# RWKV-7 chunk scan: shifted decay sum, key norm one interval ahead with a rectifier as its bound, products in halves

## What is computed

```python
kk = heads(k * k_k)
kk = kk / jnp.maximum(jnp.sqrt(jnp.sum(kk * kk, axis=-1, keepdims=True)), 1e-12)
k = k * (1.0 + (a - 1.0) * k_a)
def step(s, inp):
    r_t, w_t, k_t, v_t, aa_t, bb_t = inp          # aa = -kk, bb = kk * a
    sa = jnp.einsum('bhij,bhj->bhi', s, aa_t)
    s = s * w_t[:, :, None, :] + sa[..., None] * bb_t[:, :, None, :] + v_t[..., None] * k_t[:, :, None, :]
    return s, jnp.einsum('bhij,bhj->bhi', s, r_t)
# then per head: (y - mean) * rsqrt(var + eps) * ln_w + ln_b, plus (sum(r * k * r_k)) * v, times g, times w_o
```

## Time and profile before

| what | value |
|---|---|
| median of 3 runs | 3407.89 us (3406.33 to 3411.68) |
| the profiled execution's own time | 3415.54 us |
| its span, first to last instruction | 3413.7 us |
| mean granted PE clock | 0.965 of full |
| busy over the span | PE 90%, PEld 86%, DVE 50%, ACT 35%, POOL 29% |

### The profile page before, as it was taken

How to read it: one execution, slowest core, us unless ns; L and a number is a source line. 1 busy time by engine, 2 the same in 40 slices (tenths; PEclk the granted TensorE clock), 3 DMA queues, 4 the chain that set the end, 5 groups by cost and what they waited for, 6 DMA issues and landing times.

```text
span 3413.7 us, 73904 instructions
## 1 busy us (share of the span) xinstructions
PE 3072.6 (90%) x32214; PEld 2938.2 (86%) x32214; DVE 1694.1 (50%) x1713; ACT 1209.4 (35%) x1399; POOL 984.7 (29%) x545
## 2 busy tenths in 40 slices
PE   5999799999999997699968888887989999999996
PEld 5888699999999997699966777776979999999996
DVE  6455654544455456102116666663364445445555
ACT  4634322221222224433326777775132221112222
POOL 2222222222222223213313444444132222222221
PEclk9999899999999998799979999998999999999998
DMA  2111011111111110332231221222101111111111
GB/s 97 42 41 39 25 38 44 44 43 43 43 43 43 42 40 25 117 141 84 90 97 32 68 67 53 66 56 88 44 25 44 44 44 45 44 44 44 43 44 61
DMA packets 92154, 185.88 MB, mean 54 GB/s; under 512 B 33504, under 2 KB 56544, under 8 KB 91872
## 3 DMA queue, kind: packets, MB, share of 16 engines
q1 hardware_dynamic: 84960, 154.80, 14.5%
q10 hardware_dynamic: 6912, 26.84, 1.9%
HBM read 145.07 MB, written 36.53 MB: 53 GB/s over the span
## 4 chain that ended last, share of the span: by engine, by line
PE 75%; DVE 11%; ACT 8%; POOL 3%; issue 2%; DMA 1%; ACTq 0%; SPq 0%; DVEq 0%; POOLq 0%
PE PS L1112 66%; PE PS L1274 8%; DVE T L1543 3%; ACT T L460 2%; DVE X L1533 2%; ACT L460 2%; DVE T L1533 1%; DVE G L1533 1%; POOL HL L897 1%; DVE HL L1533 1%; ACT X L460 1%; PE PS L1230 1%; ACT UV L460 1%; POOL X L1002 1%; DVE NN L1533 1%
## 5 line engine op out<-in xcount | busy, mean ns | idle before, releaser
L897 POOL TENSOR_TENSOR WL<-RAW,WH 128x1024 fp32r<-128x1024 f32 x204 | 498.1, 2441 | 1562.4 <-ACT WH L460 1558.7
L1112 PE MATMUL PS<-HH,WH 128*128 128x364 f32 x3456 | 773.7, 332 | 79.5 <-POOL HL L897 42.2
L1112 PE MATMUL PS<-HH,WL 128*128 128x364 f32 x3456 | 769.9, 331 | 0.0
L1112 PE MATMUL PS<-HL,WH 128*128 128x364 f32 x3456 | 767.5, 331 | 0.0
L1112 PEld LDWEIGHTS PS<-HH,WH 128*128 128x128 f32 x3456 | 602.3, 190 | 94.1 <-issue 50.2
L1112 PEld LDWEIGHTS PS<-HH,WL 128*128 128x128 f32 x3456 | 608.0, 190 | 0.0
L1112 PEld LDWEIGHTS PS<-HL,WH 128*128 128x128 f32 x3456 | 606.1, 190 | 0.0
L1543 DVE SCALAR_TENSOR_TENSOR T<-T,FP 128x1092 f32<-128x1092 f32 x192 | 456.4, 2377 | 6.8
L1533 DVE TENSOR_TENSOR X<-PS,X 128x1092 f32<-128x1092 f32 x224 | 290.3, 1296 | 272.3 <-PE PS L1112 267.9
L460 ACT ACTIVATE WH<-RAW 128x1024 fp32r<-128x1024 f32 x204 | 216.6, 1062 | 408.1 <-PE PS L1112 387.7
L1112 PE MATMUL PS<-PH,WH 128*128 128x364 f32 x1344 | 301.3, 333 | 53.4 <-DVE X L1533 38.2
(11 more groups left out here) (157 smaller groups left out, 3399.6 us busy)
## 6 DMA issues: line engine op xcount, KB each, us to landing
RAW<-weights SPq DMA_DIRECT2D x204, 512.0 KB, 3.5
scratch<-T ACTq DMA_DIRECT2D x32, 546.0 KB, 2.9
scratch<-SR ACTq DMA_DIRECT2D x16, 546.0 KB, 2.9
X<-xT SPq DMA_DIRECT2D x8, 546.0 KB, 7.7
yT<-T SPq DMA_DIRECT2D x8, 546.0 KB, 2.9
T<-scratch_m SPq DMA_DIRECT2D x8, 512.0 KB, 4.1
LW<-scratch SPq DMA_DIRECT2D x16, 192.0 KB, 2.6
KK<-scratch SPq DMA_DIRECT2D x16, 192.0 KB, 2.6
```

The source lines that it names most:

```text
L897: pool.tensor_tensor(out, full, hi, ALU.subtract).then_inc(*t.made(event))
L1112: mm = pe.matmul(acc[:, j, :], a, b[:, j * CW:(j + 1) * CW], start=(i == 0 and q == 0), stop=(i == len(blocks) - 1 and q == 2))
```

## The change

- **Key norm one interval ahead.** `scaled_key`, `key_square`, `key_squares`, the lower bound, `norm_ln` and `norm_exp` work on batch job+3 (guard `has_k`) in place of job+2. All engines start at interval -3, SP at -4, loading batch job+4.
- **Its bound as a rectifier on ACT.** `floor` (DVE, max with 1e-24) becomes `above_floor` on ACT: Relu(x - 1e-24), and Ln adds the 1e-24 again.
- **Exclusive sum as a shifted inclusive one.** Z2 gets 65 columns per chunk, the first one filled with ones at the start of the scan. `removal` reads columns 0 to 63, `receptance` 1 to 64. `exclusive` on POOL and `decay_before` on ACT go.
- **Small vectors once.** PP and PQ of all pairs are loaded at the start of the program (16 DMAs); `one_less` is done once, on DVE.
- **Affine on ACT.** The scale and shift of the group norm move from DVE to ACT, after `norm_exp`.
- **Products in halves.** `solved` is cut by bank (keys, then values) with `means` between; `lower` is cut by bank with `link(4)` and `left_times(5)` between. `solved_values` waits for the new semaphore k_wv.
- **Bank 2 by its last reader.** `sums` waits for whoever read bank 2 last, in place of waits written out.
- **New orders** of the calls on all four engines; ACT's puts rectifier, Ln (key), Ln (group) and Exp (group), Exp (key) together.

The core of the diff:

```diff
-        Z2 = at("Z2", [NCH, CHUNK], o); o += PACK * 4
+        Z2 = at("Z2", [NCH, CHUNK + 1], o); o += NCH * (CHUNK + 1) * 4
...
+            for q, tile in enumerate((PP, PQ)):
+                for f in range(KT):
+                    sp.dma_start(tile[:, f, :], io["pair_vec"][q][f]).then_inc(*t.made("dma_pair"))
...
-                if job + 3 < JOBS:
-                    f, b = divmod(job + 3, NB)
-                    if job >= 0:
-                        sp.wait_ge(*t.at("k_g", 8 * (job + 1)))
-                        sp.wait_ge(*t.at("k_bonus", job + 1))
-                    sp.dma_start(PP[b][:, :], io["pair_vec"][0][f]).then_inc(*t.made(f"dma_in{b}"))
+                if job + 4 < JOBS:
+                    f, b = divmod(job + 4, NB)
+                    if job >= -1:
+                        sp.wait_ge(*t.at("k_g", 8 * (job + 2)))
+                        sp.wait_ge(*t.at("k_bonus", job + 2))
...
+                def above_floor():
+
+                    if has_k:
+                        act.wait_ge(*t.next("s_kk", 2))
+                        run(X2[:, klo:khi], PS[:, 2, 0:khi - klo], ACT.Relu, "k_max", bias=-1e-24)
...
+                def affine():
+
+                    if has_n:
+                        y = flat(Y)[:, na * CHUNK:nz * CHUNK]
+                        act.wait_ge(*t.next("k_pn"))
+                        run(y, y, ACT.Identity, "k_pt", scale=PQ[:, nf, 0:1], bias=PQ[:, nf, 1:2])
...
                 scaled_key()
                 spread_out()
-                one_less()
+                key_square()
                 key_factor()
-                key_square()
                 solved_keys()
                 solved_values()
                 decay_in()
                 turned(1)
                 growth()
+                centred_square()
+                above_floor()
                 norm_ln()
+                values()
+                turned(2)
+                group_ln()
+                group_exp()
+                turned(3)
                 norm_exp()
-                decay_before()
-                centred_square()
-                turned(2)
-                values()
-                group_ln()
-                turned(3)
-                group_exp()
+                affine()
                 keys()
                 turned(4)
                 outputs_y()
                 turned(5)
...
-                unit_plus()
-                exclusive()
-                receptance()
-                grown_key()
                 unit_key()
                 taken_key()
+                unit_plus()
                 grown_taken()
+                grown_key()
+                receptance()
                 normed()
...
                 spread()
                 powers()
-                solved()
+                solved(0)
+                means()
+                solved(1)
                 seed()
                 key_squares()
                 moves_and_left(2)
-                means()
+                fresh_out()
+                grow(2)
+                value_turn()
                 fresh_state()
-                grow(2)
-                fresh_out()
+                variances()
+                left_times(3)
                 link(0)
-                left_times(3)
+                products(0)
                 link(1)
-                value_turn()
-                variances()
-                link(2)
                 grow(3)
-                link(3)
-                products(0)
-                link(4)
-                left_times(4)
                 bonus_sums()
                 products(1)
+                link(2)
+                left_times(4)
+                key_turn()
+                link(3)
                 grow(4)
-                key_turn()
+                lower(0)
+                link(4)
+                left_times(5)
+                lower(1)
                 link(5)
-                left_times(5)
-                lower()
                 grow(5)
```

More of the change, by code:

```diff
@@ L416, in interval @@
                             sp.dma_start(dst, SE[q][:, :]).then_inc(*t.made("dma_state"))
-            for job in range(-3, JOBS - 2):
+            for job in range(-4, JOBS - 2):
                 interval(job)
@@ L738, in scaled_key @@
                 def scaled_key():
[L740 to L746, removed]
-                        run(PP[pb][:, 3:4], PP[pb][:, 1:2], ACT.Copy, "k_om", scale=-1.0, bias=1.0)
+                    if has_k:
+                        act.wait_ge(*t.next(f"dma_in{kb}", 10 if kb == NB - 1 else 5))
+                        run(X1[:, klo:khi], KK[:, klo:khi], ACT.Copy, "k_kk", scale=PP[:, kf, 0:1])
                 def key_square():
-                    if has_p:
-                        run(X2[:, lo:hi], X1[:, lo:hi], ACT.Square, "k_sq")
+                    if has_k:
+                        run(X2[:, klo:khi], X1[:, klo:khi], ACT.Square, "k_sq")
                 def spread_out():
@@ L804, in key_factor @@
                     if has_p:
-                        run(X3[:, lo:hi], AA[:, lo:hi], ACT.Identity, "k_ka", scale=PP[pb][:, 1:2], bias=PP[pb][:, 3:4])
+                        run(X3[:, lo:hi], AA[:, lo:hi], ACT.Identity, "k_ka", scale=PP[:, pf, 1:2], bias=PP[:, pf, 3:4])
                 def centred_square():
@@ L866, in interval @@
                 turned(5)
-            for job in range(-2, JOBS + 1):
+            for job in range(-3, JOBS + 1):
                 interval(job)
@@ L1260, in interval @@
                 pa, pz = BATCHES[pb]
+                ka, kz = BATCHES[(job + 3) % NB]
                 na, nz = BATCHES[(job - 1) % NB]
@@ L1914, in interval @@
                 one_more()
+                centred()
+                grown(1)
                 key()
-                grown(1)
-                weighted()
-                floor()
-                mask(2)
-                transfer()
-                centred()
-                reading()
-                grown(2)
+                mask(2)
+                reading()
+                removal()
+                grown(2)
+                transfer()
+                weighted()
                 state(0)
                 mask(3)
+                masked(0)
                 state(1)
-                removal()
+                grown(3)
+                masked(1)
                 state(2)
-                grown(3)
+                mask(4)
                 state(3)
-                masked(0)
-                mask(4)
+                grown(4)
+                bonus()
                 state(4)
-                masked(1)
-                grown(4)
-                affine()
+                mask(5)
                 state(5)
-                mask(5)
-                bonus()
-            for job in range(-2, JOBS - 1):
+            for job in range(-3, JOBS - 1):
                 interval(job)
```

128 lines of the change are left out of this document (63 added, 65 removed).

## The result

The kernel after takes 3417.47 us (median of 18 runs, 3413.39 to 3424.98), the kernel before beside it 3409.62 (18 runs, 3404.84 to 3418.19): ratio 1.0022, 95% interval 1.0015 to 1.0028. The profiled execution took 3416.91 us, its span is 3415.1. The forecast was 3382, faster; the kernel is slightly slower.

What follows compares the result with a forecast made beforehand. PE was taken to bound the kernel, busy 90%, with only the scan changing: 1.3 us less per interval over 22 intervals, 28.6, less 2.5 for filling, 26 us, so 3407.9 to 3382 us; range 3362 to 3404.

Steps and rivals of the forecast that it cites:

- What bounds the kernel now: Whole kernel: PE busy 90%; the change touches only the chunk scan (23.15 us per interval) and 16 small starting DMAs.
- First part, 12.7 us: Scan interval from its opening to the first G: 12.7 us instead of 15.81, with three PE waits and overlaps gained.
- Second part, 9.1 us: Scan interval from the first G to the next `spread`: held by DVE's chain, growing from 7.70 to 9.1 us.
- Floor and affine on ACT, two table loads less: Scan: DVE loses 0.56 and 0.48 us; ACT takes these steps but saves two table loads, 2.57 us per interval.
- The rival in which ACT holds the values: ACT's queue before the value copies: if table loads aren't saved, the interval is 0.75 us longer, 3427 us; chance 0.10.
- The gain per interval, 1.3 us: Scan: 1.3 us less than the mean interval of 23.15, over 22 intervals 28.6 us.
- `means` between the halves: Scan, first part: `means` runs between the halves of `solved`, no longer ahead of `products(0)`; gain 0.78 us.
- theory S: A follow-up's expectation for four table loads again in the scan: `products(0)` 2.5 us later, interval 2.5 us longer, ratio 1.010.
- Filling, 2.5 us: Start of the scan: more ACT work ahead delays the first products from 1776.62 to near 1779, costing 2.5 us.
- The range: Whole kernel: 3362 to 3404 us, from the larger gain to the trade, leaving out the slower case.
- a trade: Scan: the second half takes what the first gives, through DVE's longer chain; under 0.4 us per interval, 3403; chance 0.12.
- The slower case: ACT's queue between centred square and `values`: late value copies make the kernel take 3427 us; chance 0.10.

Runs made afterwards that it cites:

- p1_before_48: Kernel before with 12 small matmuls (48 PE instructions) added behind the scan; 3432.1 against 3411.8 us, ratio 1.006.
- p4_after_208: Kernel after with 52 small matmuls (208 PE instructions) added behind the scan; ratio to the kernel before 0.9955.
- b7: Kernel after with seven small matmuls (28 PE instructions) added behind the scan, nothing else; 3396.3 against 3412.4 us for the kernel before, ratio 0.9950.
- p2: Kernel after with 10 small matmuls (40 PE instructions) added behind the scan; ratio to the kernel before 0.9936.
- p3: Kernel after with 4 small matmuls (16 PE instructions) added behind the scan; ratio to the kernel before 0.9936.
- a1_affine_dve: Kernel after with seven small matmuls behind the scan and the affine moved back from ACT to DVE, behind `masked(1)`; ratio to the kernel before 0.9966.
- m2: Kernel after with seven small matmuls behind the scan and `means` put back behind `moves_and_left`; ratio to the kernel before 0.9976.
- l1: Kernel after with seven small matmuls behind the scan and `lower` in one piece again, behind `left_times(5)`; ratio to the kernel before 0.9946.

## Why the prediction was wrong

*What bounds the kernel now* said that everything the change touches lies in the scan, "so the rest is taken as unchanged". **This step failed first.** 48 added instructions moved a loop of another stage to the worst place tried: 18.5 us by the two traces, 20 us by p1_before_48, 23 us between after and p4_after_208 (1.0022 - 0.9955), whose loop is at its old place. Held, the loop gives 25 us back: 1.0022 - 0.9950 by b7, and p2 and p3 have more. None of it is in the sum. It turned the sign: with the loop at its old place the change is worth 15 us (p4), where the forecast had 26.

*First part, 12.7 us.* 13.07 in the interval that opens at 1965.47 (G's first row is at 1978.54), 12.91 in the next. Right in its steps. No wait for the value copies, none for BK: the earlier trace rows have 3.9 us for it, after has none.

```profile
1974.42 1.04 POOL L1008 TENSOR_TENSOR AR<-RR,Z 128x384 f32<-128x384 f32 x1
...
1978.54 1.23 DVE L1541 TENSOR_TENSOR G<-PS,CO 128x1024 f32<-128x1024 f32 x1 [0.47 <-PE PS L1276]
```

POOL's last product ends 10.0 us behind `spread` (10 to 11 expected, 14.5 before). The 0.55 in front of `moves_and_left` is 0.27 of issue, and the waits for UV went from 9.3 us to 0.3.

*Second part, 9.1 us.* 9.41, and the next one about 9.2. Here the reason was off: in the second part DVE itself waits for PE, 0.23 to 0.52 us at a time, so it is no pure chain of DVE, which a1_affine_dve bears out: half a microsecond more on DVE did not lengthen a steady interval. `bonus` did not wait for k_padd.

```profile
1983.54 0.49 DVE L1556 COPY M<-PS 128x320 f32<-128x320 f32 x1 [0.50 <-PE PS L1276]
1984.17 0.56 DVE L1541 TENSOR_TENSOR BON<-PS,VV 128x384 f32<-128x384 f32 x1
1985.24 0.28 DVE L1546 TENSOR_SCALAR SS<-PS,Z 128x64 f32<-128x64 f32 x1 [0.52 <-PE PS L1276]
```

*Floor and affine on ACT, two table loads less.* Right, and the rectifier needs no table of its own: two loads per interval. It takes 0.49 us on ACT, where DVE's floor took 0.56.

```profile
1972.73 0.49 ACT L461 ACTIVATE X<-PS 128x384 f32<-128x384 f32 x1
1973.24 1.28 ACT L461 ACT_TABLE_LOAD   x1
1974.53 0.53 ACT L461 ACTIVATE X<-X 128x384 f32<-128x384 f32 x1
...
1977.28 1.28 ACT L461 ACT_TABLE_LOAD   x1
1978.58 0.52 ACT L461 ACTIVATE Q<-Q 128x384 f32<-128x384 f32 x1
```

The rival in which ACT holds the values did not come about. An activation starts 0.01 to 0.02 us behind its load, so the drain of the Trainium skill (ScalarE: Activation LUTs, What ACT_TABLE_LOAD costs) is not seen here either.

*The gain per interval, 1.3 us.* Here **the second step failed**: the sum took waits off and assumed that PE would work in their stead. The waits fell by 1.37, the interval by 0.53, of which PE's idle time is only 0.11. PE's "issue" idle, 0.4 us per interval in the view of before, had no term, and became 1.6. `means` between the halves (priced at 0.78) and the halves of `lower` each bought much less than the wait they removed, 9 us for 22 intervals and nothing that can be measured, since the time came back in front of the next block of instructions ("issue" is 13 to 20 us in m2 and 21.5 in l1, against 32.6 in after). The table loads, the part with most to bring, show a third of their price: 0.86 us per interval of theory S's 2.5.

*Filling, 2.5 us.* Smaller: `products(0)` of the filling starts at 1775.64 instead of 1776.62, though everything ahead of the scan stood 1.6 us earlier in this execution, so it lost some 0.6 us.

*The range.* Its ends do not follow from their parts: a first part that gives 0.4 and a second that grows by 0.9 to 2.2 would make the interval longer, not 0.2 shorter, and 3.6 less 0.9 is 2.7, not 2.0. So the range held no slower scan, though its own parts allowed one. That the time with the loop at its old place (p4_after_208, 3398.8 us) lies inside it is partly luck.

Of the rivals *a trade* comes near the right size for the scan (0.53, where it had under 0.4), with the wrong mechanism. The slower case had a place in ACT's queue; what made the kernel slower was in none of the cases.

## What to carry to other kernels

A change that adds or removes a few instructions moves every loop behind it within its instruction blocks. When a stage that the edit does not touch gets slower, look at the gap at each jump back and count the packets of the instruction queue per turn, then try a few harmless instructions ahead of the loop: here that alone was worth 23 us of turns and 25 us of the whole. And before pricing waits of a stage with many small matmuls, divide its PE instructions by 256 and multiply by what a block costs to fetch (3.65 us here): if that is near the stage's time, a removed wait may turn into a hole that the profile calls "issue".

## What the runs showed of the hardware

- PE's instructions come in packets of 16 KB for 256 instructions, and 64x64 float32 matmuls on four quadrants use them up in 2.09 us where a new block comes each 3.65 us. The Trainium skill (Runtime: NRT & Kernel Launch, Instruction fetch mechanics) has the block of 256 and says that the cost of crossing a boundary is "mostly hidden"; in these bursts 1.4 to 1.7 us of it is not.
- The same section says that a taken branch may have to fetch its target first. The traces agree, and add that it depends on the place: 0.6 to 1.1 us of idle at each jump at place 0 (one packet ahead of it), 2.4 to 2.8 at place 47 and 3.3 to 4.3 at place 48 (two packets, one behind the other), none and no packet in any turn at places 63 to 87.
- Behind the holes of 3.3 us and more in after the granted clock stood at 0.50 for 2.9, 3.4, 5.6 and 5.1 us (at once at three jumps, 0.8 us later at the second); behind those of 0.6 to 1.1 us in before it stayed at 1.00. So a long hole costs more than its length.
- Executions of one kernel differ by 10 us, and part of it is in the scan (22.65 and 22.88 us per interval in two executions of m2). What sets it is open.
